# First unit on the raw residual in both layers, a new order of first loads and of the step sizes, and an output in blocks

## The reference, cut to what matters

```python
c_act = jax.nn.silu(c)
for l in range(DEPTH):                                   # 2 layers
    ada = c_act @ w_ada[l] + b_ada[l]                    # 1024 -> 6 * 1024
    sh1, sc1, g1, sh2, sc2, g2 = jnp.split(ada, N_ADA, axis=-1)
    h = rms_norm(x, norm1_g[l]) * (1.0 + sc1[:, None]) + sh1[:, None]
    proj = h @ w_in[l]
    z, xbc, dt_raw, q, k, v, gate_s, gate_a = split_cols(proj, IN_PROJ_WIDTHS)
    # mamba2_branch: xbc = silu(causal_dwconv(xbc)), 4 taps over time
    #                dt  = softplus(dt_raw + dt_bias), chunked scan with decays from dt
    # diff_attention_branch, gates, w_out, then an MLP of width 4096 with relu squared
    ...
return rms_norm(x, final_g)
```

## Time and profile before

| | us |
|---|---|
| median of 3 runs | 2317.55 (2314.1 to 2317.98) |
| the profiled execution | 2317.53, its span 2315.7 |
| PE busy | 2275.3 (98% of the span) |
| DVE busy | 1385.5 (60%) |
| POOL busy | 1104.6 (48%) |
| ACT busy | 1036.9 (45%) |

### The profile page before, as it was taken

How to read it: one execution, slowest core, us unless ns; L and a number is a source line. 1 busy time by engine, 2 the same in 40 slices (tenths; PEclk the granted TensorE clock), 3 DMA queues, 4 the chain that set the end, 5 groups by cost and what they waited for, 6 DMA issues and landing times.

```text
span 2315.7 us, 32199 instructions
## 1 busy us (share of the span) xinstructions
PE 2275.3 (98%) x11812; PEld 1903.1 (82%) x11812; DVE 1385.5 (60%) x2099; ACT 1036.9 (45%) x1894; POOL 1104.6 (48%) x825
## 2 busy tenths in 40 slices
PE   7999999999999999999999999999999999999997
PEld 6888998888878888888887888988888788888886
DVE  7678767556653787877777777612566436422224
ACT  2566653266653342222345665533566434432331
POOL 1466555433444454444445565554334444644442
PEclk9999999999999999999999999999999999999998
DMA  6333336422224345555432433222222232332331
GB/s 253 115 96 117 108 105 191 155 74 73 74 74 164 109 141 210 182 182 191 154 110 79 125 108 101 84 99 91 74 73 74 73 118 91 109 100 91 100 100 46
DMA packets 94126, 267.20 MB, mean 115 GB/s; under 512 B 8528, under 2 KB 35536, under 8 KB 88592
## 3 DMA queue, kind: packets, MB, share of 16 engines
q1 hardware_dynamic: 73776, 237.73, 30.3%
q10 hardware_dynamic: 20192, 27.40, 3.9%
HBM read 260.77 MB, written 4.33 MB: 114 GB/s over the span
## 4 chain that ended last, share of the span: by engine, by line
PE 72%; issue 11%; POOL 5%; POOLq 5%; DVE 4%; DVEq 1%; PEld 1%; DMA 1%; ACTq 1%; ACT 1%; SPq 0%; PEldq 0%
PE gemm L560 17%; PE gemm L562 17%; PE gemm L561 17%; POOL w_lo L1972 5%; POOLq L1974 5%; PE gemm L583 3%; PE gemm L584 3%; PE gemm L585 3%; PE aux L625 3%; PE aux L824 2%; PE aux L754 2%; PE aux L865 2%; PE aux L768 1%; PE aux L763 1%; DMA ada_pe<-stream 1%
## 5 line engine op out<-in xcount | busy, mean ns | idle before, releaser
L1972 POOL TENSOR_TENSOR w_lo<-raw,w_hi 128x512 fp32r<-128x512 f32 x704 | 972.7, 1403 | 1075.8 <-ACT w_hi L972 1067.3
L972 ACT ACTIVATE w_hi<-raw 128x1024 fp32r<-128x1024 f32 x352 | 370.8, 1058 | 669.0 <-PE gemm L562 599.0
L560 PE MATMUL gemm<-h_hi,w_hi 128*128 128x512 f32 x1456 | 584.6, 402 | 5.1 <-DVE conv L1578 4.3
L562 PE MATMUL gemm<-h_hi,w_lo 128*128 128x512 f32 x1456 | 569.8, 391 | 0.0
L561 PE MATMUL gemm<-h_lo,w_hi 128*128 128x512 f32 x1456 | 568.6, 391 | 0.0
L560 PEld LDWEIGHTS gemm<-h_hi,w_hi 128*128 128x128 f32 x1456 | 274.9, 189 | 62.1 <-issue 4.6
L562 PEld LDWEIGHTS gemm<-h_hi,w_lo 128*128 128x128 f32 x1456 | 274.1, 188 | 59.6
L561 PEld LDWEIGHTS gemm<-h_lo,w_hi 128*128 128x128 f32 x1456 | 275.0, 189 | 55.7 <-issue 1.9
L560 PE MATMUL gemm<-op_hi,w_hi 128*128 128x512 f32 x608 | 238.5, 392 | 0.3
L562 PE MATMUL gemm<-op_hi,w_lo 128*128 128x512 f32 x608 | 236.8, 389 | 0.0
L561 PE MATMUL gemm<-op_lo,w_hi 128*128 128x512 f32 x608 | 236.6, 389 | 0.0
(11 more groups left out here) (221 smaller groups left out, 3435.4 us busy)
## 6 DMA issues: line engine op xcount, KB each, us to landing
raw<-stream SPq DMA_DIRECT2D x336, 512.0 KB
ada_late<-stream SPq DMA_DIRECT2D x30, 1024.0 KB, 4.9
seg<-decay_rows ACTq DMA_DIRECT2D x64, 256.0 KB, 3.3
ada_early<-stream ACTq DMA_DIRECT2D x40, 256.0 KB, 4.0
raw<-stream SPq DMA_DIRECT2D x32, 256.0 KB
ada_first<-stream SPq DMA_DIRECT2D x5, 1024.0 KB, 20.8
x<-xT SPq DMA_DIRECT2D x2, 2048.0 KB, 10.2
ada_pe<-stream SPq DMA_DIRECT2D x3, 1024.0 KB, 14.1
```

The costliest lines, as they stand in the source:

```text
L560: mm(o, w_hi[:, slot, k, cols], hi[:, k, :], start=k == 0, stop=False)
L562: last = mm(o, w_lo[:, slot, k, cols], hi[:, k, :], start=False, stop=k == KB - 1)
L972: A(w_hi[:, slot, ks], raw[:, slot, ks], ACT.Copy).then_inc(hi_ready, 1)
L1972: gp.tensor_tensor(w_lo[:, slot, ks], raw[:, slot, ks], w_hi[:, slot, ks].bitcast(F32), ALU.subtract)
```

## The change

It does five things. In layer 0 unit 0 also multiplies `x * scale` ahead of the norm, with `shift_column` on PE for the shift's share. The four scale pieces are fetched first, then parameters, unit 0 and x, then the shift pieces; three pieces that PE and DVE still have to sum are taken behind unit 0. In both layers `conv_seed(0)` writes the corrected result back to its PSUM bank and the taps read it there; the bank comes free with the last tap. In both layers the ticks of `taps(0)`, `silu(0)`, `taps(1)` and `steps_of_dt` change, and `sums_of_dt` moves on PE by a tick. At the end, the last square goes to PE by itself, ACT scales `y_out` ahead, and DVE multiplies by rstd in blocks of 2, 2, 2, 1 and 1, with five transfers.

```diff
-FIRST, FIRST_PE = [(0, m) for m in (0, 1, 2, 3, 7)], [(0, m) for m in (4, 5, 6)]
+FIRST, FIRST_PE = [(0, m) for m in (4, 5, 6, 0, 1)], [(0, m) for m in (7, 2, 3)]
+N_SCALE = 3
+OUT_PARTS = [slice(0, 2), slice(2, 4), slice(4, 6), slice(6, 7), slice(7, 8)]
...
# SP
+            piece(ada_first[0], *FIRST[0], first_in[0])
+            piece(ada_pe[0], *FIRST_PE[0], pe_in[0])
+            for n in range(1, N_SCALE):
                 piece(ada_first[n], *FIRST[n], first_in[n])
+            load_par(0)
+            load(0, 0, 0)
+            sp.dma_start(x[:], xT).then_inc(x_in, 16)
+            load(0, 0, 1)
+            load_dtw(0)
+            for n in range(1, len(FIRST_PE)):
+                piece(ada_first[N_SCALE + n - 1], *FIRST[N_SCALE + n - 1], first_in[N_SCALE + n - 1])
+                piece(ada_pe[n], *FIRST_PE[n], pe_in[n])
...
# PE
+                def shift_column(j):
+
+                    for k in range(KB):
+                        last = mm(ab[0][:, TB + j:TB + j + 1], raw[:, 0, k, j * P:(j + 1) * P], ada_v[:, 0, k:k + 1],
+                                  start=k == 0, stop=k == KB - 1)
+                    return last
...
                 if l == 0:
+                    pe.wait_ge(pe_in[0], 16)
+                    ada_piece(ada_pe[0], ab[3], 2 * FIRST_PE[0][1])
+                    for n in range(N_SCALE):
+                        ada_column(n, ada_acc, ab[3], 2 * FIRST[n][1], 2, N_FIRST)
+                    pe.drain().then_inc(scale_out, 1)
...
+                unit(l, 0, xs_top, xs_lo, before_top)
+                if l == 0:
+                    pe.wait_ge(pe_in[1], 16)
+                    ada_piece(ada_pe[1], ab[3], 2 * FIRST_PE[1][1])
+                    norm_spread(st)
                     pe.wait_ge(pe_in[2], 16)
                     ada_piece(ada_pe[2], ab[3], 2 * FIRST_PE[2][1])
-                    norm_spread(st)
-                    for n in range(1, N_FIRST):
+                    for n in range(N_SCALE, N_FIRST):
                         ada_column(n, ada_acc, ab[3], 2 * FIRST[n][1], 2, N_FIRST)
                     pe.drain().then_inc(ada_full, 1)
+                    pe.wait_ge(ada_read, 1)
+                    shift_column(0)
...
-                    if l == 0 and k < KB - 1:
-                        mid_part(k)
-                    if l and k in (1, 3):
+                    if l == 0 and k == 0:
+                        shift_column(1).then_inc(top_acc, 1)
+                    if k in (1, 3, 5):
                         mid_part(KB + k // 2)
...
                     if tick == T_FIRST + 2:
-                        if l:
-                            at += 2
-                        at = fill(at, 2)
+                        at = fill(at + 3, 1)
                         x_to_tokens()
-                        if l == 0:
-                            at = fill(at, 2)
...
-                    if tick == T_FIRST + 4:
-                        sums_of_dt()
...
+                    if tick == T_FIRST + 5:
+                        sums_of_dt()
                     early(tick)
# ACT
-                    source = gb[c][:]
-                    if l and n == 0:
-                        act.wait_ge(top_scaled, 2 * (l - 1) + j + 1)
-                        A(raw_bc[:, j], raw_bc[:, j], ACT.Identity, bias=fbias[:, j:j + 1])
+                    if n == 0:
+                        act.wait_ge(top_scaled, 2 * l + j + 1)
+                        A(gb[c][:], raw_bc[:, j], ACT.Identity, bias=fbias[:, j:j + 1])
...
# DVE
+            def top_low(l, k):
+
+                dve.wait_ge(top_hi, l * KB + k + 1)
+                STT(xs_lo[:, k], x[:, k], amul[:, k:k + 1], xs_top[:, k].bitcast(F32),
+                    ALU.mult, ALU.subtract).then_inc(top_lo, 1)
...
-                    if l and tick == T_FIRST + 2:
+                    if tick == T_FIRST + 1:
+                        taps(0, 0)
+                        taps(0, 1)
+                    if tick == T_FIRST + 3:
+                        silu(0, 0)
+                        silu(0, 1)
+                        taps(1, 0)
+                        taps(1, 1)
                         steps_of_dt()
...
-            norm_mean(last_step, True)
-            norm(last_step, lambda k: con[:, K_FG + k:K_FG + k + 1], None)
+            b = full(last_step, 0)
+            TS(ms[:], b[:, 0:TB], 1.0 / D, EPS, ALU.mult, ALU.add)
+            b = full(last_step, 2)
+            settle()
+            STT(ms[:], b[:, 0:TB], 1.0 / D, ms[:], ALU.mult, ALU.add)
+            dve.drain().then_inc(S_["ms"], 1)
+            dve.wait_ge(y_scaled, KB)
+            b = full(last_step, 1)
+            for ks in OUT_PARTS:
+                TT(y_out[:, ks], y_out[:, ks], b[:].unsqueeze(1).broadcast_to([P, ks.stop - ks.start, S]), ALU.mult)                    .then_inc(y_done, 1)
# POOL
-                    rsqrt_of_x(st)
                     low_unit(l, 0)
+                    rsqrt_of_x(st)
                     low_unit(l, 1)
```

More of the change, by code:

```diff
@@ L233, in build @@
         w_lo = place("w_lo", [P, 2, KB, UW], F32R, r_lo)
-        h_hi = place("h_hi", [P, KB, S], F32R, region(K16))
-        h_lo = place("h_lo", [P, KB, S], F32R, region(K16))
+        r_h = region(2 * K16)
+        h_hi = place("h_hi", [P, KB, S], F32R, r_h)
+        h_lo = place("h_lo", [P, KB, S], F32R, r_h + K16)
         r_op = region(2 * K16)
@@ L521, in sp_program @@
                     load_dtw(l + 1)
-            for k in range(KB):
-                sp.wait_ge(S_["pre"], DEPTH * TOTAL["pre"] + k + 1)
-                sp.dma_start(out[:, k], y_out[:, k]).then_inc(out_done, 16)
-            sp.wait_ge(out_done, KB * 16)
+            for n, ks in enumerate(OUT_PARTS):
+                sp.wait_ge(y_done, n + 1)
+                sp.dma_start(out[:, ks], y_out[:, ks]).then_inc(out_done, 16)
+            sp.wait_ge(out_done, len(OUT_PARTS) * 16)
         def pe_program(pe):
@@ L958, in pe_program @@
                 st.end()
-            norm_sum(Step(DEPTH, "start"))
-            norm_spread(Step(DEPTH, "start"))
+            st = Step(DEPTH, "start")
+            norm_sum(st)
+            b = aux(st, 2)
+            pe.wait_ge(S_["sq"], st.at("sq", KB - 1) + 1)
+            for t in range(TB):
+                last = mm(b[:, t:t + 1], sq[:, (KB - 1) % 2, t * P:(t + 1) * P], ones[:, 0:1], start=True, stop=True)
+            last.then_inc(aux_full[2], 1)
+            pe.wait_ge(S_["rs"], st("rs") + 1)
+            b = aux(st, 1)
+            for t in range(TB):
+                last = mm(b[:, t * P:(t + 1) * P], rs[:, t:t + 1].broadcast_to([P, P]), ident, start=True, stop=True)
+            last.then_inc(aux_full[1], 1)
         def act_program(act):
@@ L996, in squares_of_x @@
                         A(xs_hi[:, k], x[:, k], ACT.Copy, scale=amul[:, KB + k:KB + k + 1]).then_inc(S_["xs_hi"], 1)
+                    if scaled == "out":
+                        A(y_out[:, k], x[:, k], ACT.Copy, scale=con[:, K_FG + k:K_FG + k + 1]).then_inc(y_scaled, 1)
                     if scaled == "top":
@@ L1020, in act_program @@
             act.wait_ge(ready, 1)
+            convert(0, 0, 0)
             act.wait_ge(x_in, 16)
+            act.wait_ge(scale_in, 1)
+            for k in range(KB):
+                A(xs_top[:, k], x[:, k], ACT.Copy, scale=amul[:, k:k + 1]).then_inc(top_hi, 1)
+            convert(0, 0, 1)
             squares_of_x(Step(0, "start"), range(KB), False)
@@ L1344, in act_program @@
                             squares_of_x(st_next, range(2 * (u - 4), 2 * (u - 4) + 2),
-                                         scaled="top" if l + 1 < DEPTH else None)
+                                         scaled="top" if l + 1 < DEPTH else "out")
                         if u < 4:
@@ L1465, in norm @@
                         STT(dst, x[:, k], mul(k), b[:], ALU.mult, ALU.mult).then_inc(S_["pre"], 1)
-                        if k == KB - 1 and step.phase != "mix" and not 0 < step.layer < DEPTH:
-                            dve.drain().then_inc(aux_free[1], 1)
                     if k and shift is not None:
@@ L1576, in taps @@
                         w = block * CONV + CONV - 1 - lag
-                        source = raw_bc[:, j, 0:S - lag] if l and n == 0 else gb[c][:, 0:S - lag]
-                        last = STT(conv[:, c, lag:S], source, cw[:, w:w + 1], conv[:, c, lag:S], ALU.mult, ALU.add)
-                        if lag == CONV - 1 and (l == 0 or n):
+                        last = STT(conv[:, c, lag:S], gb[c][:, 0:S - lag], cw[:, w:w + 1], conv[:, c, lag:S], ALU.mult, ALU.add)
+                        if lag == CONV - 1:
                             last.then_inc(bank_free[n % 2], 1)
```

156 lines of the change are left out of this document (75 added, 81 removed).

## The result

The changed kernel takes 2333.76 us (2332.39 to 2334.83, 6 runs) against 2317.24 us (2314.10 to 2318.20, 6 runs) before: ratio 1.0075, 95% interval 1.0065 to 1.0086. It is slower by 16.5 us, where 9.7 were forecast, and lies just above the range (2333.5). The profiled execution of after is its fastest, 2332.39 us with a span of 2330.6. Span against span the change costs 14.9 us. PE is still busy 98% of the span, so the whole difference must again be in PE's waits, its clock or its work.

What follows compares the result with a forecast made beforehand. PE, busy 98% of the span, was taken as the bound, so only its waits, clock and work count. Layer 0 +13.1, layer 1 -1.5 and the end -1.9 gave +9.7 on 2317.5: 2327 us, 8-in-10 range 2314.5 to 2333.5.

Steps and rivals of the forecast that it cites:

- layer 0, at the turn of the dt rows: Layer 0 on PE: dt rows turned at 105.5 us instead of 92.41, a loss of 13.1 us that nothing gives back.
- layer 1, to its turn: Layer 1 on PE: same work in another order, turn at 1234.9 instead of 1236.41, so -1.5 us.
- the end: After the last product: last addition off the path, sums of squares and DVE's blocks cheaper, together -1.9 us (-0.5 to -3.3).
- Unit 0 … 37.4: Layer 0, unit 0 on PE: starts at 22.7 us, 48 products plus the sum of squares, ends at 37.4.
- The new wait: PE ahead of `sums_of_dt`: waits 4.8 us in layer 0, 5.0 in layer 1 for DVE's step sizes, then lower clock.
- Taps from PSUM: Unit 0's taps in both layers: same pace from PSUM, ACT's write 0 +- 0.2 us four times, taken as 0.
- The clock stays up through the one-column stretch: Rival, 13%: behind unit 0 in layer 0 one-column matmuls keep the upper clock; layer 0 only +0.6, total 2314.7 us.
- A wait under 2.5 us: Rival, 8%: step sizes take 6.8 us, PE's wait for them stays short and the clock up; total 2317.2 us.
- All at the dear end: Rival, 9%: step sizes take 11.2 us in both layers and piece 2 takes 6.9; total 2333.9 us.

Runs made afterwards that it cites:

- Holding POOL back: Changed kernel with one more wait on POOL, so unit 0's first `w_lo` comes only after the scale is written: 2332.54 us, ratio 1.0070.
- the split version: Changed kernel with PE's shift pieces 2 and 3 cut in halves, three of the four halves between blocks of unit 0: 2327.19 us, ratio 1.0057.
- the pieces between the blocks and late sums: Changed kernel with halved PE pieces between unit 0's blocks and the sums of dt behind four parts of unit 3: 2316.95 us, ratio 0.9999.
- late sums: Changed kernel with `sums_of_dt` on PE behind four parts of unit 3 and `dt_to_tokens` behind six, both layers: 2319.05 us, ratio 1.0014.
- SBUF version: Changed kernel with the corrected result of unit 0 kept in `raw_bc` and its taps read from SBUF: 2330.92 us, ratio 1.0060.

## Why the prediction was wrong, step by step

The direction and the mechanism were right, and a size was off. In us of the span, the term was forecast and measured as follows:

| term | forecast | measured |
|---|---|---|
| layer 0, at the turn of the dt rows | +13.1 | +16.6 |
| from there to the sums in layer 1's unit 0 | 0 | +1.2 |
| layer 1, to its turn | -1.5 | -1.6 |
| from there to the last product | 0 | -0.1 |
| the end | -1.9 | -1.2 |
| sum | +9.7 | +14.9 |

The medians differ by 16.5 us, 1.6 more than the profiled executions do, mostly because the one of after was the fastest of its runs. Of the 6.8 us between 2327 and 2333.8, then, 3.5 lie in layer 0, 1.2 between the layers and 0.7 at the end.

**The failed step is "Unit 0 … 37.4".** It ended at 41.84, 4.4 us late, and three things make up 4.3 of this:
- Start: 24.36 instead of 22.7, 1.7 us. I costed DVE's third scale piece at 4.0, and had `w_lo` of the same half ready "by 20" without asking what it does to DVE. The piece took 5.4. Holding POOL back showed it.
- Squares: the wait was 1.92 us instead of 0.5, 1.4 more. DVE's copy takes 1.10 us and its seven additions 6.31, beside POOL's second `w_lo` (28.73 to 31.46). In the kernel before, with POOL idle, they took 0.43 and 5.39. That POOL is the cause was not tested here.
- Clock: 48 products were costed as 5.4 us at the lower clock and the rest at the upper. But the last six ran 0.43 us apart again, 0.2 more each, 1.2 us. Why the clock fell there stays open: two profiles with a wait of 1.8 us at the same place show no fall in unit 0, and the two of the split version show one with no wait at all. This part came back behind unit 0, where the clock rose again. Moving the sum by one block was worth 4.8 us of the median (3.9 by the ratio), by the idle and by what then ran at the upper clock behind unit 0.

From there on the steps hold, each a little shorter than forecast, 1.2 us in all up to the shift. Piece 2 4.0 us (4.0), spread 1.55 (2.05), piece 3 6.83 (6.9), `shift_column(0)` at 56.12 (52.9), the first dt product at 59.55 (56.4). Unit 2 starts at 83.62 (80.3), and the lag stays at 3.2 to 3.4. The step sizes took 9.75 us from 90.93 (9.3), the wait 5.61 (4.8), the sums 1.89 (1.8), and the turn came 3.5 us behind the forecast.

**The new wait** was the largest term and is confirmed by its removal. The forecast for the spread of the step sizes came out of the same contention. The Trainium skill's page "SBUF — State Buffer" ("Who interferes with whom") gives the rule that was quoted ahead, that DVE with two SBUF inputs and a reading GpSimd hold each other up. Here the trace agrees: 1.30 against 0.29 us for a small instruction, 5.37 against 3.61 for a piece, 7.75 against 4.93 for six taps. I had applied the rule to the step sizes alone, when it also bore on the scale piece and on `xs_lo`.

**Layer 1** came out as forecast, -1.6: 4.3 us waited for a tap became 5.6 for the step sizes. What the new layer 1 is worth without its wait, 7 us of the span, shows only once the sums stand later.

**Taps from PSUM** were put at 0, because taps on `raw_bc` and on `gemm` had the same pace before. That reading missed what POOL did: while the kernel before took its taps from `raw_bc` (1216.57 to 1221.6), POOL had nothing to do (1214.8 to 1224.65), so the equal pace said nothing of such taps beside POOL. There the six taps differ by 2.8 us, but the step sizes behind them give that back, and the time can't be told from 0.

**The end**: the gains were there (one addition less, the last sum in 1.02 us instead of 1.87, DVE 0.7 shorter). The spread took 2.07 us as before (2.08), and the transfers took 1.0 back where I had 0.3.

**The rivals.** *The clock stays up through the one-column stretch* is refuted for the kernel after (6.83 us for piece 3, windows at 0.60 and 0.50). But in the profiled run with the pieces between the blocks and late sums (2312.9, one of four such among eleven) the clock was down from 39 to 42 (0.52) and then read 1.00 up to 48, through both halves and the spread. So a part of what the rival needs can happen. *A wait under 2.5 us* is refuted by 5.6. *All at the dear end*, 2333.9, came nearest in the number, for other reasons: it had 11.2 us for the step sizes, which took 9.75, and 6.9 for piece 2, which took 4.0.

One reading of the forecast was off without effect: the granted clock of 0.71 that it puts after the 4.3 us idle belongs to the last 2 us of that idle (1226 to 1228; PE restarted at 1228.08).

What stays open: the 1.2 us between layer 0's turn and layer 1, of which the list of waits there shows 0.7 in small ones. And at what moment the clock rises and falls in unit 0: with starts of unit 0 within 0.1 us of each other it rose at about 27, 28.6 and 30 us in three of the profiles above. It isn't known what decides this.

## What to carry to other kernels

When a chain is moved behind other work on one engine, move its consumer on the waiting engine by the same amount; here one edit of that kind on PE was worth some 14 us of the 16.5 that the change had cost. Before costing an instruction by a row, ask what the other engines do beside it in the new order, for both the moved work and the work that it lands on. On an engine that is busy 98%, place each small dependent instruction so that its input is surely there: moving one by a block, where it waited 1.9 us, was worth about 4 us. And before a fall of the clock is put down to a wait, look at a second profile with the same wait.

## What the runs showed of the hardware

- Dense one-column matmuls did not hold the upper clock here: with PE busy all 5 us of 45 to 50 the granted clock was 0.60, and then 0.50. A record took 0.216 us at 1.2 GHz and about 0.11 at 2.4 (1.84 us for 16).
- A wait of 1.9 us with one-column sums behind it was followed by the lower clock inside dense 512-column products in the kernel after (39 to 42: 0.54). Waits of 1.78 and 1.82 us at the same place were not (late sums, POOL held back), and in both profiles of the split version it fell there with no wait. Behind a wait of 1.9 us ahead of the sums of dt it stayed up (SBUF version, 104 to 108: 1.00). Waits of 3.0 and 5.6 us were followed by the lower clock each time.
- One program has times some 5 us apart: 2311.4 to 2312.9 and 2315.7 to 2318.4 us in the split version with late sums, eleven runs, with a lower mean clock in the slower ones. In which stretch it is lower isn't shown.
- DVE instructions with two SBUF inputs beside POOL's `w_lo`: 5.37 us against 3.61 for seven 256-column products; taps from PSUM beside the same work kept 0.82 us each.
